# An encoder block on one core: the next head's transposes moved ahead of the value products in each attention step

## The chip, the core and the metric

The kernel runs on one core of a Trainium2 chip. Its time is the device time of one execution in microseconds; smaller is better. A core has TensorE (matmuls and transposes), VectorE, ScalarE, GpSimd and queues that issue DMAs; they run side by side and wait for one another by semaphores. In the profile TensorE is PE (its weight loads PEld), VectorE DVE, ScalarE ACT, GpSimd POOL, and the queue of the sync engine SP.

## What is computed

One layer of a bidirectional encoder over two request groups (1024 and 256 tokens, width 1024, all float32), each attending to itself alone:

```
p = rmsnorm(x) @ w_in                         # uv, c_q, c_kv, k_rope, gate_A, gate_B
A = chunked gMLP of uv;  B = attention of 8 heads from c_q, c_kv, k_rope
    s = q @ k.T * 192**-0.5;  prob = softmax(s);  o = prob @ v        # per head
x = x + (sigmoid(gate_A) * A + sigmoid(gate_B) * B) @ w_out
x = x + expert_choice_ffn(rmsnorm(x))         # 16 experts
```

A head has 128 plain and 64 rotated dimensions for queries and keys and 128 for values. The change concerns the attention alone.

## The kernel before

Every product is made in float32 precision from two parts of each operand, a high one (rounded) and a low one (what the rounding left): three matmuls, high by high, high by low and low by high. So each operand that comes out of a transpose is copied by ScalarE (high part), and VectorE subtracts this from the original in PSUM (low part).

The attention stage is a loop of 84 steps, written out by hand in the same order on each engine; the engines' orders are fixed. Step n belongs to head h = n // 10 and to the query chunk of 128 tokens ORD[s], s = n % 10, with ORD = (0, 1, 2, 3, 8, 9, 4, 5, 6, 7). Chunks 0 to 7 are the first group, with 1024 keys; 8 and 9, at s = 4 and 5, are the second, with 256. In one step TensorE does, in this order:

- `scores(n)`: the scores of step n, ten matmuls of 512 columns (five of 256 at s = 4 and 5), lines L1235 to L1239, into banks 0-1 or 2-3 of PSUM. It waits for the exponential of step n - 2, and at s = 0 for all pieces of its head.
- `turn_prob(n - 2)`: eight transposes (two for a chunk of the second group) of the probabilities of step n - 2, L1248, into bank 4 on. It waits for GpSimd's normalisation of step n - 2 (norm_pool) and for VectorE's low part of step n - 3 (pt_lo_dve).
- `values((n - 4) // 2, n % 2)`: half of the value products of a pair of chunks, 12 matmuls of 256 columns (3 for the pair of the second group, at s = 8 and 9), L371 to L373, into bank 6. The first half waits for the pair's low parts and for the copy of the pair before.
- `turn_head(9 * (h + 1) + s)` for s up to 8 and all heads but the last: one of nine pieces of the next head's queries and keys, two or four transposes, L1181, from the tile tok. All of them write bank 7, so each waits until the high and the low part of the piece before have been made (x_hi, x_lo). s = 0 to 2 are the queries, 3 to 5 the keys, 6 to 8 the rotated parts of both.

After the last step of a head's pieces (s = 8) the SP queue loads tok with the queries (L623) and keys and values (L626) of the head after.

ScalarE in one step: `high(n - 2)`, the high part of the transposed probabilities (L1797); `expo(n)`, the exponential with its sum (L1807); at odd steps `out_pair`, the copy of a finished pair of value products (L1814); then `high_head`, the high part of the step's piece (L1761, for rotated ones L1764, L1765 and L1767).
VectorE: `top(n)`, maximum and bias of the scores (L2173, L2175); `low(n - 2)`, the low part of the transposed probabilities (L2182); `inverse(n)`, the reciprocal of the sum (L2188); then `low_head`, the low part of the step's piece (L2131, for rotated ones L2136 and L2138).
GpSimd: the normalisation of the probabilities (L877) from the reciprocal, and at s = 4 the splitting of the next head's values.

Of the kernel before, what the change touches and what calls it, by code (L numbers as in the profile page):

```python
# [33 lines left out]
H = 8  # L34
# [24 lines left out]
PIECES = 9  # L59
# [30 lines left out]
def piece(x):  # L90

    return (0, 2, 1)[x // 3], 4 * (x % 3), (4, 4, 2)[x % 3]
# [22 lines left out]
def keys(c):  # L115
    return (0, TP) if c < NCH_P else (TP, TS)


def build(nc, x_p, x_s, norm1_g, w_in, v_norm_g, w_spatial, b_spatial, w_a_out, q_norm_g, w_uq,
# [3 lines left out]
    with ctx:  # L123
# [24 lines left out]
        def bank(b, n=BANK, w=1):  # L148
            return PS[:, b * BANK:b * BANK + n * w]
# [145 lines left out]
        with ExitStack() as s:  # L295
# [3 lines left out]
            with ExitStack() as s2:  # L299
                sb(s2, "act_room", [P, 2, KD, T])  # L300
                s = s2
# [4 lines left out]
            with ExitStack() as s2:  # L306
                s = s2
# [154 lines left out]
        def x_bank(x):  # L462
            return bank(6 + x % 2 if x < PIECES else 7)
# [525 lines left out]
        def _(pe):  # L989
# [177 lines left out]
            def turn_head(x):  # L1167

                h, i = divmod(x, PIECES)
                kind, c0, cn = piece(i)  # L1170
                pe.wait_ge(S["tq_in"], 16 * (h + 1))
                if kind > 0:
                    pe.wait_ge(S["tkv_in"], 16 * (h + 1))
                free = x - 1 if h == 0 else x
                if h == 0:
                    pe.wait_ge(S["pa_copy"], UNITS)
                if free > 0:
                    pe.wait_ge(S["x_hi"], free)
                    pe.wait_ge(S["x_lo"], free)
                for c in range(cn):  # L1180
                    last = pe.transpose(x_bank(x)[:, c * P:(c + 1) * P],  # L1181
                                        tok[:, c0 + c, (0, NOPE, HEAD + ROPE)[kind]:][:, 0:P], ident[:])
                last.then_inc(S["x_pe"], 1)
# [34 lines left out]
            def scores(n):  # L1218
                h, s = divmod(n, NCH)
                hd, c = heads[h % 2], ORD[s]  # L1220
                k0, kn = keys(c)
                if s == 0:
                    if h < 2:
                        pe.wait_ge(S["krl_zero"], h + 1)
                    pe.wait_ge(S["x_hi"], PIECES * (h + 1))
                    pe.wait_ge(S["x_lo"], PIECES * (h + 1))
                if n > 1:
                    pe.wait_ge(S["exp_act"], n - 1)
                else:
                    pe.wait_ge(S["evac"], 3 * G_B - (3 if n == 0 else 0))  # L1230
                q = slice(c * P, (c + 1) * P)
                for o in range(0, kn, BANK):
                    w = min(BANK, kn - o)
                    out, k = bank(s_bank(n) + o // BANK, w), slice(k0 + o, k0 + o + w)
                    pe.matmul(out, hd["q_hi"][:, q], hd["k_hi"][:, k], start=True, stop=False)  # L1235
                    pe.matmul(out, hd["q_hi"][:, q], hd["k_lo"][:, k], start=False, stop=False)  # L1236
                    pe.matmul(out, hd["q_lo"][:, q], hd["k_hi"][:, k], start=False, stop=False)  # L1237
                    pe.matmul(out, hd["qr2"][:, q], hd["kr2"][:, k], start=False, stop=False)  # L1238
                    last = pe.matmul(out, hd["qr2"][:, q], hd["krl"][:, k], start=False, stop=True)  # L1239
                last.then_inc(S["scores_pe"], 1)  # L1240

            def turn_prob(n):
                kn = keys(ORD[n % NCH])[1]
                pe.wait_ge(S["norm_pool"], n + 1)
                if n > 0:
                    pe.wait_ge(S["pt_lo_dve"], n)
                for k in range(kn // P):
                    last = pe.transpose(bank(4, kn)[:, k * P:(k + 1) * P], prob[:, n % 3, k * P:(k + 1) * P], ident[:])  # L1248
                last.then_inc(S["probT_pe"], 1)

            def values(pr, half):
                h = pr // 5
                hd = heads[h % 2]
                k0, kn = keys(ORD[2 * (pr % 5)])
                ks = kn // P // 2
                if half == 0:
                    pe.wait_ge(S["pt_lo_dve"], 2 * pr + 2)
                    if pr % 5 == 0:
                        pe.wait_ge(S["v_lo_pool"], h + 1)
                    if pr > 0:  # L1260
                        pe.wait_ge(S["values_act"], pr)
                for k in range(half * ks, (half + 1) * ks):
                    v = slice(k0 + k * P, k0 + (k + 1) * P)
                    last = mm3(pe, bank(6, 2 * P), hd["v_hi"][:, v], hd["v_lo"][:, v], pt_hi[:, pr % 2, k],
                               pt_lo[:, pr % 2, k], k == 0, k == 2 * ks - 1)
                if half:
                    last.then_inc(S["values_pe"], 1)

            def b_row(j, k):

                if k == 0:
                    pe.wait_ge(S["w_split"], G_B + j + 1)
                    pe.wait_ge(S["exp_act"], STEPS)
                    if j == 1:
                        pe.wait_ge(S["pt_lo_dve"], STEPS)
                pe.wait_ge(S["part_lo"], at("part_lo", KD + k + 1))
                for b, (t0, tn) in enumerate(BLOCKS):
                    last = mm3(pe, lin_set(j, b), w_hi[:, j, k], w_lo[:, j, k], o_hl[:, k, 0, t0:t0 + tn],
                               o_hl[:, k, 1, t0:t0 + tn], k == 0, k == KD - 1)
                    if k == KD - 1:  # L1280
                        last.then_inc(S["tile_pe"], 1)

            for n in range(STEPS + 4):
                h, s = divmod(n, NCH)
                if n < STEPS:
                    scores(n)
                if 2 <= n < STEPS + 2:
                    turn_prob(n - 2)
                if n >= 4:
                    values((n - 4) // 2, n % 2)  # L1290
                if h < H - 1 and s < PIECES:
                    turn_head(PIECES * (h + 1) + s)
                if n >= STEPS:
                    b_row(0, n - STEPS)
            for k in range(4):
# [1202 lines left out]
```

## Time and profile before

| | |
|---|---|
| time, median of 3 runs | 2140.59 us (2136.91 to 2142.15) |
| span of the profiled execution, first to last instruction | 2139.5 us (no other time of it is given) |
| TensorE busy | 2098.5 us, 98% of the span |
| VectorE, ScalarE, GpSimd busy | 57%, 44%, 31% |
| attention stage | about 752 to 1112 us |

Times in the profile are counted from the start of the span. Busy time is the time in which an engine executes; matmuls overlap one another in the records, so a matmul's own duration is longer than the distance to the next. The chain that ended last is better for distances: there each piece begins where the work moves on to it. The granted clock is the share of TensorE's full speed (2.4 GHz) that it was given in a stretch; the lower of its two levels is 1.2 GHz. "<-" in a row of a tile stands between what is written and what is read; [0.28 <-PE ...] at the end of a row is the idle time before it and who ended it.

### The profile page before, as it was taken

How to read it: one execution, taken by the hardware profiler on the slowest of the kernel's cores; microseconds unless marked ns; L12 is line 12 of the kernel's file. 1: busy time of each engine (PE TensorE's matmuls, PEld its weight loads, DVE VectorE, ACT ScalarE, POOL GpSimd, SP SyncE). 2: the span in 40 equal slices, each digit the busy share in tenths (PEclk: the TensorE clock that was granted, in tenths of full speed). 3: DMA queues.
4: the chain of work that ended last, by engine and by line, in shares of the span. 5: the costliest groups of instructions: out<-in, count | busy, mean ns of one | idle time of the engine just before them, and what ended most of it. 6: DMA issues, size and time to landing. Idle time of an engine off the chain costs nothing.

```text
span 2139.5 us, 33534 instructions
## 1 busy us (share of the span) xinstructions
PE 2098.5 (98%) x13424; PEld 1727.8 (81%) x13424; DVE 1222.6 (57%) x1434; ACT 939.8 (44%) x1180; POOL 670.2 (31%) x434
## 2 busy tenths in 40 slices
PE   8999999999999999999999999899999999999997
PEld 8888888888888888888888888677777777777775
DVE  5344601222385567777654438966667676666764
ACT  5112311211455366666640022355555555555553
POOL 2333222212355366766642510221121111112111
PEclk9999999999999999999999999999999999999999
DMA  5122223544676642213134432588788887877883
GB/s 180 54 88 87 71 103 121 167 131 146 209 262 235 214 143 84 67 65 114 40 101 150 169 119 92 226 341 315 282 292 298 292 311 289 310 286 288 300 291 94
DMA packets 185270, 397.41 MB, mean 186 GB/s; under 512 B 16736, under 2 KB 104800, under 8 KB 185184
## 3 DMA queue, kind: packets, MB, share of 16 engines
q1 hardware_dynamic: 170592, 343.78, 45.1%
q0 software_dynamic: 7680, 20.98, 4.0%
q10 hardware_dynamic: 6912, 31.46, 3.7%
q8 instruction: 60, 0.98, 0.2%
q14 instruction: 26, 0.21, 0.0%
HBM read 317.53 MB, written 78.64 MB: 185 GB/s over the span
## 4 chain that ended last, share of the span: by engine, by line
PE 88%; DVE 7%; ACT 2%; DMA 1%; issue 1%; POOL 0%; SPq 0%; ACTq 0%; DVEq 0%; POOLq 0%
PE PS L1441 25%; PE PS L371 14%; PE PS L372 14%; PE PS L373 14%; PE PS L1472 8%; PE PS L1248 2%; DVE small L2173 1%; PE PS L1235 1%; PE PS L1239 1%; PE PS L1238 1%; PE PS L1236 1%; PE PS L1237 1%; PE PS L1181 1%; ACT prob L1807 1%; PE PS L1140 1%
## 5 line engine op out<-in xcount | busy, mean ns | idle before, releaser
L371 PE MATMUL PS<-act_hi,w_hi 128*128 128x512 f32 (+1 forms) x1072 | 382.7, 357 | 0.3 <-DVE act_lo L1980 0.2
L373 PE MATMUL PS<-act_hi,w_lo 128*128 128x512 f32 (+1 forms) x1072 | 375.5, 350 | 0.0
L372 PE MATMUL PS<-act_lo,w_hi 128*128 128x512 f32 (+1 forms) x1072 | 375.2, 350 | 0.0
L877 POOL TENSOR_SCALAR prob<-prob,small 128x1024 f32<-128x1024 f32 (+1 forms) x80 | 200.4, 2505 | 120.9 <-DVE small L2188 120.9
L371 PEld LDWEIGHTS PS<-act_hi,w_hi 128*128 128x128 f32 x1072 | 202.7, 189 | 27.0 <-issue 0.7
L373 PEld LDWEIGHTS PS<-act_hi,w_lo 128*128 128x128 f32 x1072 | 202.4, 189 | 27.2
L372 PEld LDWEIGHTS PS<-act_lo,w_hi 128*128 128x128 f32 x1072 | 202.9, 189 | 25.2 <-issue 0.7
L780 POOL TENSOR_SCALAR w_hi<-w_raw 128x1024 fp32r<-128x1024 f32 x46 | 49.4, 1074 | 418.5 <-PE PS L373 391.5
L1441 PE MATMUL PS<-ehi,xT_hi 128*128 128x512 f32 x520 | 167.9, 404 | 0.6 <-DVE xT_lo L2370 0.4
L1441 PE MATMUL PS<-elo,xT_hi 128*128 128x512 f32 x520 | 160.8, 390 | 0.0
L1441 PE MATMUL PS<-ehi,xT_lo 128*128 128x512 f32 x520 | 160.6, 390 | 0.0
L947 POOL DMA_INDIRECT y_s<-ob_s,ixs_s x16 | 44.0, 2751 | 354.4 <-DVE ob_s L2456 354.4
L2402 DVE TENSOR_TENSOR elo<-raw,ehi 128x2048 fp32r<-128x2048 f32 x65 | 147.4, 2286 | 11.3 <-ACT ehi L1902 11.3
L1902 ACT ACTIVATE ehi<-raw 128x2048 fp32r<-128x2048 f32 x68 | 129.7, 1911 | 25.6 <-PE PS L1441 16.8
L2051 DVE SCALAR_TENSOR_TENSOR yt<-PS,small,bb 128x512 f32<-128x512 f32 (+1 forms) x24 | 15.9, 662 | 214.2 <-PE PS L1140 214.2
L782 POOL TENSOR_TENSOR w_lo<-w_raw,w_hi 128x1024 fp32r<-128x1024 f32 x46 | 124.7, 2712 | 3.8
L1441 PEld LDWEIGHTS PS<-ehi,xT_hi 128*128 128x128 f32 x520 | 92.4, 188 | 35.3 <-issue 13.2
L2402 DVE TENSOR_TENSOR elo<-raw_w,ehi 128x2048 fp32r<-128x2048 f32 x32 | 72.0, 2289 | 79.4 <-ACT ehi L1902 79.3
L1441 PEld LDWEIGHTS PS<-elo,xT_hi 128*128 128x128 f32 x520 | 97.6, 188 | 21.2
L1441 PEld LDWEIGHTS PS<-ehi,xT_lo 128*128 128x128 f32 x520 | 97.6, 188 | 21.0
L1797 ACT ACTIVATE pt_hi<-PS 128x1024 fp32r<-128x1024 f32 (+1 forms) x80 | 71.9, 898 | 88.8 <-PE PS L1248 87.7
L1628 ACT ACTIVATE stg<-PS 128x512 f32<-128x512 f32 (+1 forms) x48 | 25.3, 527 | 178.3 <-PE PS L373 178.2
(344 smaller groups left out, 4812.2 us busy)
## 6 DMA issues: line engine op xcount, KB each, us to landing
raw<-in_w_gate SPq DMA_DIRECT2D x64, 1024.0 KB, 10.5
raw_more<-in_w_up SPq DMA_DIRECT2D x32, 1024.0 KB, 6.8
raw_w<-in_w_up SPq DMA_DIRECT2D x32, 1024.0 KB, 10.7
w_raw<-in_w_in SPq DMA_DIRECT2D x35, 512.0 KB, 4.0
w_raw<-in_w_down SPq DMA_DIRECT2D x15, 1024.0 KB, 5.0
stg<-in_w_down SPq DMA_DIRECT2D x15, 1024.0 KB, 7.0
gt<-in_w_down SPq DMA_DIRECT2D x15, 1024.0 KB, 11.5
raw_end<-in_w_down SPq DMA_DIRECT2D x15, 1024.0 KB
```

What stands on the lines that cost most here:

```text
L371: pe.matmul(out, lh, rh, start=first, stop=False)
L372: pe.matmul(out, lh, rl, start=False, stop=False)
L373: return pe.matmul(out, ll, rh, start=False, stop=last)
L780: pool.tensor_scalar(w_hi[:, j], w_raw[:, j], 1.0, 0.0, ALU.mult, ALU.add).then_inc(S["w_rounded"], 1)
L782: pool.tensor_tensor(w_lo[:, j], w_raw[:, j], f32(w_hi[:, j]), ALU.subtract).then_inc(S["w_split"], 1)
L877: pool.tensor_scalar(prob[:, n % 3, 0:kn], prob[:, n % 3, 0:kn], prec[:, s:s + 1], None, ALU.mult).then_inc(S["norm_pool"], 1)
L947: pool.indirect_dma_start(y_quarters, bass.IndirectOffsetOnAxis(ap=ixs_s[:, 0:1], axis=0), ob_s[:], None, compute_op=ALU.add).then_inc(S[" ...
L1441: last = pe.matmul(bank(b0 + half), lhs[:, k], rhs[:, pt, kin, half * BANK:(half + 1) * BANK], start=st, stop=sp_)
L1472: last = pe.matmul(bank(bs)[CAP_S * g:CAP_S * (g + 1), 0:GN], few(k), raws[slot][:, k % 2, g * GN:(g + 1) * GN], start=(k == 0), stop=(k = ...
L1797: act.activation(pt_hi[:, pr % 2, 0:kn // P, o:o + P], bank(4, kn).rearrange("p (k q) -> p k q", q=P), ACT.Copy).then_inc(S["pt_hi_act"], 1)
L1902: act.activation(ehi[:, pt], raws[slot], ACT.Copy).then_inc(S["e_hi"], 1)
L2402: dve.tensor_tensor(elo[:, pt], raws[slot], f32(ehi[:, pt]), ALU.subtract).then_inc(S["e_lo"], 1)
```

## The change

In each step `turn_head` is issued directly behind `turn_prob`, ahead of `values`, instead of behind it. Nothing else is changed: the orders of ScalarE, VectorE, GpSimd and the queues are the same, and so are all waits, buffers and sizes.

```diff
                 if 2 <= n < STEPS + 2:
                     turn_prob(n - 2)
+                if h < H - 1 and s < PIECES:
+                    turn_head(PIECES * (h + 1) + s)
                 if n >= 4:
                     values((n - 4) // 2, n % 2)
-                if h < H - 1 and s < PIECES:
-                    turn_head(PIECES * (h + 1) + s)
                 if n >= STEPS:
                     b_row(0, n - STEPS)
```

## Rows read from the trace of the kernel before

**Rows 1.** The page: the span, busy us of each engine (share) xinstructions.

```profile
span 2139.5 us, 33534 instructions
...
PE 2098.5 (98%) x13424; PEld 1727.8 (81%) x13424; DVE 1222.6 (57%) x1434; ACT 939.8 (44%) x1180; POOL 670.2 (31%) x434
```

**Rows 2.** Busy us by stretch: PE, PEld, DVE, ACT, POOL, then granted clock, DMA.

```profile
830.00:870.00 40.00, 39.85 (x272) 35.62 (x271) 29.65 (x49) 26.59 (x46) 27.14 (x12) 1.00 0.35 109
...
1070.00:1080.00 10.00, 8.53 (x69) 8.03 (x67) 6.93 (x12) 7.06 (x12) 6.02 (x3) 1.00 0.26 80
...
1095.00:1100.00 5.00, 3.45 (x21) 3.48 (x22) 2.58 (x3) 2.63 (x5) 3.85 (x2) 0.75 0.44 134
1100.00:1105.00 5.00, 5.00 (x33) 4.55 (x33) 0.73 (x1) 1.39 (x3) 0.00 (x0) 0.91 0.07 27
```

**Rows 3.** The chain that ended last, 804 to 819 us: start, us, what.

```profile
804.58 0.87 PE PS L1248 x8
...
812.73 1.06 PE PS L1248 x8
...
815.23 0.44 PE PS L1181 x4
...
816.26 1.06 PE PS L1248 x8
...
818.76 0.22 PE PS L1181 x2
```

**Rows 4.** The same chain, 824 to 840 us.

```profile
827.34 0.44 PE PS L1181 x4
...
830.08 0.87 PE PS L1248 x8
...
831.31 0.30 PE PS L1181 x2
...
833.91 0.99 PE PS L1248 x8
...
835.25 0.36 PE PS L1235
...
837.82 1.07 PE PS L1248 x8
```

**Rows 5.** Timeline of VectorE, 791 to 838 us: start, us, instruction.

```profile
803.54 0.75 DVE L2131 SCALAR_TENSOR_TENSOR q_lo<-PS,small,q_hi 128x512 fp32r<-128x512 f32 x1 [0.69 <-ACT q_hi L1761]
...
813.40 0.75 DVE L2131 SCALAR_TENSOR_TENSOR k_lo<-PS,small,k_hi 128x512 fp32r<-128x512 f32 x1 [0.69 <-ACT k_hi L1761]
...
814.89 1.22 DVE L2182 TENSOR_TENSOR pt_lo<-PS,pt_hi 128x1024 fp32r<-128x1024 f32 x1 [0.16 <-ACT pt_hi L1797]
...
816.42 0.75 DVE L2131 SCALAR_TENSOR_TENSOR k_lo<-PS,small,k_hi 128x512 fp32r<-128x512 f32 x1 [0.24 <-ACT k_hi L1761]
...
825.35 0.69 DVE L2138 TENSOR_TENSOR krl<-PS,kr 64x512 fp32r<-64x512 f32 x1
...
830.36 0.69 DVE L2138 TENSOR_TENSOR krl<-PS,kr 64x512 fp32r<-64x512 f32 x1
...
834.62 0.43 DVE L2138 TENSOR_TENSOR krl<-PS,kr 64x256 fp32r<-64x256 f32 x1
...
836.46 1.21 DVE L2182 TENSOR_TENSOR pt_lo<-PS,pt_hi 128x1024 fp32r<-128x1024 f32 x1
```

**Rows 6.** Timeline of ScalarE, 791 to 838 us.

```profile
812.67 0.70 ACT L1761 ACTIVATE k_hi<-PS,small 128x512 fp32r<-128x512 f32 x1
...
815.70 0.69 ACT L1761 ACTIVATE k_hi<-PS,small 128x512 fp32r<-128x512 f32 x1 [0.28 <-PE PS L1181]
```

**Rows 7.** Timeline of the SP queue, 740 to 1110 us.

```profile
831.64 0.52 SPq L623 DMA_DIRECT2D tok<-q_d  x1
...
1005.73 0.52 SPq L623 DMA_DIRECT2D tok<-q_d  x1
```

**Rows 8.** DMA issues, 831 to 838 us: count, KB each, us to landing.

```profile
tok<-q_d SPq DMA_DIRECT2D x1, 960.0 KB, 5.5
```

## The prediction

> **What bounds the kernel now.** I read the page first: TensorE is busy for 98% of a span of 2139.5 us [rows 1]. So the change can pay only where TensorE waits inside the attention stage (about 752 to 1112 us), and costs where it puts a wait into a full TensorE. The table by stretch comes next: from 830 to 870 us TensorE was busy for 39.85 of 40 us at a granted clock of 1.00, while VectorE had 29.65 and ScalarE 26.59 us [rows 2]. There is almost nothing to win there. But the other engines' handovers can lie close to TensorE's needs, which an average doesn't show, so I followed the chain of work through one head (h = 1, 796 to 840 us) and put beside it the timelines of VectorE and ScalarE. "Step s" is the position in the head, n = 10h + s; P are the transposes of the probabilities, V the value products, T the next head's transposes, S the scores.
>
> In the chain a row starts when TensorE's work moves on to it. Eight transposes take 0.87 us, four T 0.44, two T 0.22 [rows 3, 4]. The V of step 5 fills 817.32 (816.26 + 1.06) to 818.76, 1.44 us for 12 matmuls; a V of the small pair, steps 8 and 9, fills 830.95 (830.08 + 0.87) to 831.31, 0.36 us.
>
> A handover from VectorE to a transpose is to be seen at step 5: the low part of the probabilities ended at 814.89 + 1.22 = 816.11 [rows 5], P began at 816.26 and took 1.06 instead of 0.87 us [rows 3]. So from the end of the producer to the place from which normal pace counts it is 0.15 + 0.19 = 0.34 us. At step 0 of the next head: 836.46 + 1.21 = 837.67, P from 837.82 with 1.07 us [rows 4, 5], 0.35. I use 0.34.
>
> **The change part by part.** No instruction is added or removed, no bytes, no buffer. T moves past V: 12 matmuls, 3 at steps 8 and 9 (step 9 has no T), and nothing at steps 0 to 3 of head 0, where there is no V. TensorE's sum per step stays: P + T + V + S has the same parts. What moves is the moment at which T's waits must be met: T of step s waits until VectorE has written the low part of the piece before (x_lo), because all pieces share one PSUM bank. Until now V's 1.43 us lay ahead of that wait as cover; now only P does. V behind T waits for low parts that P's own wait has met already, and for the copy of the pair before; both are done. The SP queue: the load of the next head's queries starts when T of step 8 is done, and T of step 0 needs it. It was issued at 831.64, about 5.5 us to landing [rows 7, 8], so some 837.1; T will stand behind P of step 0, which ends at 837.82 + 1.07 = 838.89 [rows 4]. Still covered by 1.7 us. T of the key kinds needs the second load only from step 3. At step 2 T may begin at 803.54 + 0.75 + 0.34 = 804.63 [rows 5], and P ends at 804.58 + 0.87 = 805.45 [rows 3]; of the steps 0 to 3 this has the least to spare. ScalarE and GpSimd: the copy of T's result comes behind the exponential of its step, and at odd steps behind the copy of V's result too, so a T that ends earlier gives ScalarE little: at step 3 the copy of the keys (812.67) follows without a gap behind ScalarE's own work [rows 6]. V ends later by T's 0.22 to 0.44 us, and nothing waits closely for it.
>
> Now the sum for one head. The low part of a piece ends at 813.40 + 0.75 = 814.15 (step 3), 816.42 + 0.75 = 817.17 (step 4), 825.35 + 0.69 = 826.04 (step 6), 830.36 + 0.69 = 831.05 (step 7), 834.62 + 0.43 = 835.05 (step 8) [rows 5].
>
> Step 4. P ends at 812.73 + 1.06 = 813.79, where T now wants to begin. It may at 814.15 + 0.34 = 814.49. New wait: 0.70 us. Before, T stood at 815.23 [rows 3], later than 814.49, so V hid the wait with 0.74 us to spare. This low part is late because ScalarE's copy was, whose input was there long before; so moving T of step 3 earlier doesn't mend it.
>
> Step 5. T of step 4 now ends at 814.93. Its copy began at 815.70, for which ScalarE had idled 0.28 us [rows 6], and can begin some 0.3 us earlier; its low part earlier by the 0.24 us that VectorE idled for it [rows 5], 816.93. TensorE is late by 0.70, so P can start at 816.26 + 0.70 = 816.96, when the low part that it waited for (816.11, plus 0.34) is long there: its 1.06 shrinks to 0.87. I round what it gives back to 0.20; shift after P: 0.70 - 0.20 = 0.50. P ends at 817.32 + 0.50 = 817.82, and T may begin at 816.93 + 0.34 = 817.27: no new wait. Everything behind, the scores, maxima and exponentials of steps 6 and 7 too, is now late by 0.50.
>
> Step 7. P ends where V began, 827.34 - 1.43 = 825.91, with the shift 826.41. T may begin at 826.04 + 0.50 + 0.34 = 826.88. New wait: 0.47; shift 0.97. The low part of step 7 hangs on the exponential and on VectorE's order, not on this wait, so it stays late by 0.50 only.
>
> Step 8. P ends at 830.95 + 0.97 = 831.92, T may begin at 831.05 + 0.50 + 0.34 = 831.89: no new wait. T took 0.30 instead of 0.22 us [rows 4], which falls away: shift 0.89. Step 9: P took 0.99 instead of 0.87: shift 0.77. Step 0: the first score product took 0.36 us instead of 0.23, a tenth of the 2.30 from 831.61 (831.31 + 0.30) to 833.91; it waits for the last low part. Shift 0.64. Then P of step 0: TensorE is ready at 837.68 + 0.64 = 838.32 (835.25 + 0.36 + 9 x 0.23 = 837.68), the low part at 837.67 + 0.50 + 0.34 = 838.51: the old wait shrinks from 0.33 to 0.19 us, and the shift becomes 0.50 again. So the wait of step 7 is paid back by the tail of the head, where VectorE's chain sets the pace, and what remains of a head is step 4's wait less what step 5 gives back: 0.70 - 0.20 = 0.50 us. The head repeats: the query loads stand at 831.64 and, four heads later, at 1005.73, 43.52 us apart each [rows 7]. T is issued in the heads 0 to 6, and steps 4 to 8 exist with V in all seven: 7 x 0.50 = **3.5 us**.
>
> Bounds. Step 4's wait: not under 0 (it is hidden if the copy comes 0.7 us earlier than I think), and at most 0.70 with nothing given back, 4.9 us in all. Steps 4 and 7 with nothing given back: 7 x (0.70 + 0.47) = 8.2 us. All places where T's cover shrinks below its need, singly and with nothing given back: 0.70 at step 4, at step 5 what is short from the old times, 817.17 + 0.34 - 817.32 = 0.19, at step 7 826.38 - 825.91 = 0.47, at step 8 831.39 - 830.95 = 0.44 less the 0.08 of today: 1.72 x 7 = 12.0 us. The waits of V (two semaphores, at even steps) now stand behind only two to four transposes. The trace has no such place; the nearest is S behind two transposes with one wait, and there T's row is the plain 0.22 us [rows 3], with no gap behind it. I take nothing; at the upper end a slow first product of 0.19 us as above, at 4 even steps with T behind P and V in each head, 7 x 4 x 0.19 = 5.3 us. A gain: at most the waits of today, 0.20 + 0.20 + 0.08 + 0.12 + 0.13 + 0.33 = 1.06 us in a head (steps 4, 5, 8, 9 and 0), 7.4 us if all go and none comes; step 4's own is ahead of T, and takes 1.4 of it off.
>
> The clock. At step 4 TensorE will do, between the scores and V (P began at 812.73 [rows 3]), only transposes or nothing: 1.05 + 0.70 + 0.44 = 2.19 us. The trace holds a fall: between 1095 and 1100 us the granted clock averages 0.75, between 1100 and 1105 0.91, and of the first of them TensorE was busy for 3.45 of 5 us; between 1070 and 1080, with 1.47 us idle in two waits, it stayed at 1.00 [rows 2]. 0.75 and 0.91 mean 2.5 + 0.9 us at the lower level (1.2 GHz), which cost half of that, 1.7 us. The Trainium skill (page "TensorE: Matmul & The Clock Gate", Part 4: PE-mode transpose) says that the full clock does not engage for transposes, which speaks against lining up P, the wait and T; by that rule the sum would be the clock rival's below. The row from 1070 to 1080 speaks for 3.5 us, the fall shows that the rival is not impossible.
>
> **The rivals.**
> A (forecast): one new wait of 0.70 us at step 4 and one of 0.47 at step 7, the latter absorbed: +3.5 us, 2144.1. Chance 0.60.
> B: hidden anyway. ScalarE's copies come earlier with T and no low part is late: 2140.6. For it speaks the 0.28 us idle of ScalarE at step 4; against it that at step 3 ScalarE isn't waiting for T. 0.13.
> C: nothing is absorbed, or V's waits show. +8.2 to +12.0 us, 2148.8 to 2152.6. For it: the margins are tenths of a microsecond. Against: the tail of each head waits for VectorE today. 0.15.
> D: the clock falls once per head at step 4: 3.5 + 7 x 1.7 = 15.4, 2156.0. 0.05.
> E (the other side): the pieces finish earlier and VectorE's backlog at the head's end, where the low parts of step 8 end at 835.05 only and hold the scores and P of step 0, is gone, with no new wait: 7 x (0.08 + 0.12 + 0.13 + 0.33) = 4.6 us, 2136.0. It decides from the point where the copy at step 8 follows T, not the exponential, and where step 3's low part ends before 813.45. Against it: both rows say otherwise. 0.07.
>
> **How the numbers follow.** The sum was made against the profiled execution (span 2139.5 us; no other time of it is given), 1.1 us under the median of the three runs, 2140.59; 2139.5 + 3.5 = 2143.0, and carried over to the median 2144.1. The runs shown differ by 5.2 us, so the median of a few may be off by some 2 us. The range 2138.0 to 2151.5 takes in A, B and most of C; outside are D, most of E and the end of C. About 0.3% (6.4 us) is what a measurement of this kernel tells from no change. A and B are inside it but for a small part of A on the slow side; of C most is beyond, D wholly; of E hardly anything by its own price. Faster 0.03, the same 0.78, slower 0.19.
>
> **What would show it.** In the profile of the changed kernel: TensorE idle ahead of T, released by the low part of the keys, at step 4 of each of seven heads for about 0.7 us and at step 7 for about 0.45; none at steps 0 to 3, 5 and 6; P of step 5 back at 0.87 us; query loads some 44.0 us apart instead of 43.52; clock 1.00 throughout; no wait of T on the query load. The prediction is wrong if T waits at step 4 are absent (B), if the heads are 44.6 us or more apart (C), if the clock falls (D), or if they are under 43.4 apart (E).

## The result, and the profile after

The changed kernel takes 2145.28 us (median of 11 runs, 2142.30 to 2147.08), the kernel before 2140.47 us (11 runs): a ratio of 1.0023, interval 1.0015 to 1.0030, so 3.2 to 6.4 us slower. Run again beside the kernel before in a later set of runs (e8) it was 1.0028 (1.0019 to 1.0037). Forecast were +3.5 us and 2144.1.

The loads of the next head's queries (SP queue: start, us) mark the heads:

```profile
792.55 0.52 SPq L623 DMA_DIRECT2D tok<-q_d  x1
...
836.56 0.52 SPq L623 DMA_DIRECT2D tok<-q_d  x1
...
1012.63 0.52 SPq L623 DMA_DIRECT2D tok<-q_d  x1
```

From 836.56 to 1012.63 lie four heads of 44.02 us; before they were 43.52 us apart [rows 7]. So a head takes 0.50 us longer, and seven make 3.5 us. The whole stage says the same. From the first of its query loads to a store near its end, before and then after, are 332.22 and 335.64 us, 3.4 us more:

```profile
747.72 0.52 SPq L623 DMA_DIRECT2D tok<-q_d  x1
...
1079.94 0.32 SPq L639 DMA_DIRECT2D o_d<-ostg  x1
```

```profile
751.65 0.52 SPq L623 DMA_DIRECT2D tok<-q_d  x1
...
1087.29 0.32 SPq L639 DMA_DIRECT2D o_d<-ostg  x1
```

The distance of the heads is a far finer gauge than the time of the kernel: it is a difference inside one execution, between places that the rest of the kernel doesn't touch.

Where the half microsecond is, the timeline of the head shows that [rows 3 to 6] show (h = 1; start, us, instruction, idle before it and its end). First step 4:

```profile
817.07 0.70 ACT L1761 ACTIVATE k_hi<-PS,small 128x512 fp32r<-128x512 f32 x1
817.13 1.06 PE L1248 MATMUL PS<-ident,prob 128*128 128x128 f32 x8
...
817.80 0.75 DVE L2131 SCALAR_TENSOR_TENSOR k_lo<-PS,small,k_hi 128x512 fp32r<-128x512 f32 x1 [0.69 <-ACT k_hi L1761]
...
818.69 0.63 PE L1181 MATMUL PS<-ident,tok 128*128 128x128 f32 x4 [0.50 <-DVE k_lo L2131]
```

P ends at 817.13 + 1.06 = 818.19. The low part of step 3's piece ends at 817.80 + 0.75 = 818.55, 0.36 us later, and T begins at 818.69 after 0.50 us of idle TensorE, and then takes 0.63 us where it took 0.44 [rows 3]. Together 0.50 + 0.19 = 0.69 us, on a TensorE that had none of it before. The chain that ended last then goes on so (start, us, what):

```profile
818.69 0.63 PE PS L1181 x4
...
821.35 0.87 PE PS L1248 x8
...
822.23 0.22 PE PS L1181 x2
...
831.08 0.63 PE PS L1181 x4
...
835.43 0.87 PE PS L1248 x8
...
836.31 0.22 PE PS L1181 x2
...
839.17 0.87 PE PS L1248 x8
...
840.40 0.23 PE PS L1235
...
842.49 0.23 PE PS L1239
842.71 1.06 PE PS L1248 x8
...
843.77 0.44 PE PS L1181 x4
```

Line by line against [rows 3, 4]: P of step 5 is back from 1.06 to 0.87 us. T of step 7 takes 0.63 instead of 0.44, a wait. T of step 8 is back from 0.30 to 0.22, P of step 9 from 0.99 to 0.87. The first score product of the next head is back from 0.36 to 0.23. P of step 0 is still a waiting one with 1.06, but it follows the last score product without a gap (842.49 + 0.23), where 0.13 us lay before (837.69 to 837.82). Together 0.08 + 0.12 + 0.13 + 0.13 = 0.46 us, nearly all that step 7's wait had cost.

All seven heads do the same, as the table of who waited for whom over the stage (752 to 1118 us; us in total, times, longest) says. None of the L1181 rows is in the table of before:

```profile
PE PS L1181 <- DVE k_lo L2131: 3.5, 7, 0.5
PE PS L1181 <- DVE krl L2138: 2.0, 7, 0.3
```

Seven waits of 0.50 for the keys' low part (step 4), and seven of 0.28 for that of the rotated parts (step 7). The slower first transposes, 0.19 each, come on top.

Outside the stage the two profiled executions differ for another reason. The query load at the stage's beginning stands at 751.65 instead of 747.72, 3.9 us late before any edited instruction has run. In the table by stretch (busy us of PE, PEld, DVE, ACT, POOL, then the granted clock and DMA) the changed kernel's execution has

```profile
300.00:310.00 10.00, 10.00 (x52) 8.24 (x51) 0.00 (x0) 1.16 (x3) 0.00 (x0) 0.83 0.01 2
600.00:610.00 10.00, 8.25 (x35) 7.42 (x36) 6.96 (x20) 6.66 (x15) 1.27 (x2) 0.83 0.77 263
1095.00:1105.00 10.00, 7.89 (x51) 6.75 (x50) 7.08 (x10) 7.11 (x12) 7.98 (x4) 1.00 0.06 19
```

and that of before

```profile
300.00:310.00 10.00, 10.00 (x63) 8.61 (x62) 0.00 (x0) 1.75 (x4) 0.00 (x0) 1.00 0.01 2
600.00:610.00 10.00, 8.55 (x44) 7.08 (x43) 4.84 (x15) 5.66 (x12) 1.08 (x2) 1.00 0.73 251
1095.00:1105.00 10.00, 8.45 (x52) 8.03 (x53) 3.31 (x4) 4.02 (x8) 3.85 (x2) 0.83 0.26 80
```

A mean of 0.83 over 10 us is 3.4 us at the lower level (1.2 GHz), an estimated 1.7 us lost. Such a fall comes at 304 and 602 us in one execution, at 1097 us in the other. The same DMA issues in both executions, taken as marks, say what they came to. The changed kernel's are level with the others before 304 us, 1.6 us late behind it, 3.9 late at the stage's beginning, 7.35 late at the store near its end (1079.94 and 1087.29), and 5.8 late behind the fall of the kernel before, from 1105 us on. So 5.9 us between the spans (2145.4 to 2139.5) are not 5.9 us of the change: 3.4 to 3.5 are. And some 0.7 us of the 3.9 are more than the two falls make; e8 below comes back to them.

### The profile page after: what moved, and what is told of

It reads as the page before. It is cut to its first block, busy times and chain, and to the rows that moved or that the text cites. A ratio compares the mean times of both kernels' runs of the same rounds, so it can differ in the third digit from the quotient of the medians.

```text
span 2145.4 us, 33534 instructions
## 1 busy us (share of the span) xinstructions
PE 2099.2 (98%) x13424; PEld 1729.3 (81%) x13424; DVE 1225.6 (57%) x1434; ACT 940.2 (44%) x1180; POOL 672.5 (31%) x434
## 4 chain that ended last, share of the span: by engine, by line
PE 89%; DVE 5%; ACT 2%; issue 1%; DMA 1%; POOL 0%; SPq 0%; ACTq 0%; DVEq 0%; POOLq 0%
PE PS L1441 25%; PE PS L371 14%; PE PS L372 14%; PE PS L373 14%; PE PS L1472 8%; PE PS L1248 2%; PE PS L1239 1%; PE PS L1236 1%; PE PS L1238 1%; PE PS L1235 1%; PE PS L1237 1%; PE PS L1181 1%; ACT prob L1807 1%; PE PS L1140 1%; DMA stg<-ya_d 1%
```

## The experiments

Each theory says what the heads' distance must be. Theory A is the prediction's: step 4's wait is paid, less 0.20 us that step 5 gives back, and step 7's is taken back by the tail of the head. Rival C says that waits add up. Rival O, that the order costs in every step (V behind T's waits, transposes in a row).

**Step 4 alone** (e1_only_4)

```diff
-                if n >= 4:
-                    values((n - 4) // 2, n % 2)
-                if h < H - 1 and s < PIECES:
+                first = s == 4
+                if first and h < H - 1 and s < PIECES:
+                    turn_head(PIECES * (h + 1) + s)
+                if n >= 4:
+                    values((n - 4) // 2, n % 2)
+                if not first and h < H - 1 and s < PIECES:
                     turn_head(PIECES * (h + 1) + s)
```

> The next head's transposes stand ahead of the value products at step 4 of each head alone. Theory A (only step 4's wait is paid): TensorE waits about 0.6 to 0.7 us ahead of them for the keys' low part, step 5 gives 0.20 back, and the query loads of successive heads lie 44.0 us apart, as in the changed kernel (44.02; 43.52 before), +3.5 us in all. Rival C (waits add up, step 7's 0.47 is paid too): without step 7 the distance must be shorter than the changed kernel's, 43.8 or less. Rival O (the order itself costs a little in every step): of 0.50 us in a head about a ninth, distance 43.6.

Measured (SP queue):

```profile
832.59 0.52 SPq L623 DMA_DIRECT2D tok<-q_d  x1
...
1008.57 0.52 SPq L623 DMA_DIRECT2D tok<-q_d  x1
```

Four heads of 43.995 us: one of nine moves brings 0.47 of the 0.50 us (ratio 1.0010, 1.0001 to 1.0020). That rules out C (43.8 or less) and O (43.6).

**All but steps 4 and 5** (e2_not_4_5): the same edit with `first = s not in (4, 5)`.

> The changed order in all steps but 4 and 5. Theory A: no wait at steps 4 and 5; at step 7 TensorE still waits some 0.3 to 0.5 us ahead of the next head's transposes, but the tail of the head takes it back (the wait ahead of the probabilities' transposes at step 0 shrinks), so the query loads lie 43.52 us apart as before, and the time is that of the kernel before within 1 us. Rival C (the wait at step 7 is paid): 44.0. Rival O (the order itself costs): seven ninths of the cost stay, 43.9.

Measured: loads from 831.64 to 1005.85, 43.55 us apart; ratio 0.9997 (0.9987 to 1.0006). And yet TensorE waits in each head, for as long as in the changed kernel:

```profile
PE PS L1181 <- DVE krl L2141: 2.0, 7, 0.3
```

A wait seven times in the table, and 0.03 us of it in the heads' distance: the time is missing from the waits behind it. The chain through the head of [rows 4] has T of step 7 with its wait, then T of step 8 and P of step 9 at their quick 0.22 and 0.87 us:

```profile
826.16 0.63 PE PS L1181 x4
...
831.40 0.22 PE PS L1181 x2
...
834.27 0.87 PE PS L1248 x8
```

**Step 5 alone** (e3_only_5): `first = s == 5`.

> The changed order at step 5 alone. Theory A: the low part of step 4's piece ends at 817.17 and 0.34 later, at 817.51, the transposes may begin; the probabilities' transposes end at 817.32: a wait of 0.19 us that nothing takes back, query loads 43.7 us apart, +1.3 us. Rival B (such small waits vanish in the slack of the other engines): 43.5 us apart. Rival O: about a ninth of the cost, 43.6.

Measured: loads from 833.58 to 1008.28, 43.68 us apart, so 0.16 us in a head, against 0.19 expected. T of step 5 shows it, 0.41 us where [rows 3] have 0.22:

```profile
819.11 0.41 PE PS L1181 x2
```

It is 1.1 us in all, which the time doesn't show (0.9998, 0.9988 to 1.0007).

**The changed order without the shared bank** (e4_own_banks), on the changed kernel:

```diff
         def x_bank(x):
+            if x >= PIECES and x % PIECES in (4, 5):
+                return bank(1 if x % PIECES == 4 else 3)
             return bank(6 + x % 2 if x < PIECES else 7)
...
                 free = x - 1 if h == 0 else x
+                if h > 0 and i in (4, 5, 6):
+                    free = PIECES * h + 4 if i == 6 else 0
...
+                if h < H - 1 and s in (6, 7):
+                    pe.wait_ge(S["x_hi"], PIECES * (h + 1) + s - 1)
+                    pe.wait_ge(S["x_lo"], PIECES * (h + 1) + s - 1)
```

> The changed order in all steps, but the pieces of steps 4 and 5 are written to the PSUM banks 1 and 3, which the short scores of these two steps leave free, so they need not wait for the piece before; the scores of steps 6 and 7 wait instead until these banks have been read. Nothing else differs from the changed kernel. Theory A (the shared bank's wait at step 4 is the whole cost): no wait ahead of these transposes at step 4, query loads 43.5 us apart, the time of the kernel before within 1 us. Rival O (what costs is the order on TensorE, such as the value products behind transposes with their own waits, not the bank): 44.0 us apart, +3.5 us.

Measured: loads from 831.90 to 1005.87, 43.49 us apart; ratio 0.9996 (0.9986 to 1.0006). The wait for k_lo is gone and the cost with it; that for krl (7 times, 2.0 us) stays, unpaid. So it is the one PSUM bank of all pieces that makes the changed order dear. A row that I had not expected, of the weight loads, in the same table:

```profile
PEld PS L1185 <- DMA tok<-q_d: 0.4, 1, 0.4
```

T waited once for the load of its queries, which took 7.3 us; the head from 788.05 to 831.90 is 43.85 us long.

**ScalarE's order, on the changed kernel** (e5_copy_first)

```diff
+                ahead = s % 2 == 1
+                if ahead and h < H - 1 and s < PIECES and n > 0:
+                    high_head(PIECES * (h + 1) + s)
                 if n % 2 and 5 <= n:
                     out_pair((n - 5) // 2)
-                if h < H - 1 and s < PIECES and n > 0:
+                if not ahead and h < H - 1 and s < PIECES and n > 0:
                     high_head(PIECES * (h + 1) + s)
```

> The changed kernel, and at odd steps ScalarE makes the high part of the next head's piece ahead of the copy of the pair's value products instead of behind it. At step 3 the copy of the value products takes about 0.27 us ahead of the keys' high part (812.40 to 812.67 before). Theory A: the keys' low part of step 3 is done 0.27 us earlier, so step 4's wait shrinks from about 0.70 to 0.43 us; further 0.1 us comes back at the tail, where steps 5 and 7 have the same copy. Query loads 43.6 to 43.7 us apart instead of 44.02, +1.4 us to the kernel before. Rival B (the low part is late for another reason, VectorE's order): 44.0, +3.5 us.

Measured: loads from 834.12 to 1008.75, 43.66 us apart; ratio 1.0010 (1.0000 to 1.0019).

```profile
PE PS L1181 <- DVE k_lo L2134: 1.9, 7, 0.5
```

The waits for the keys' low part fell from 3.5 to 1.9 us, 0.23 each. So the copy of the value products, 0.27 us ahead of the high part, is one of the things that make this low part late. The chain of the changed kernel shows the whole of it, ScalarE's exponential, copy and high part in a row:

```profile
815.62 0.97 ACT prob L1807
...
816.71 0.20 ACT prob L1807
816.91 0.27 ACT ostg L1814
817.18 0.59 ACT k_hi L1761
```

**Steps 7 and 8 of the kernel before** (e6_order_by_step): T ahead of V with `first = s == 8`, the high part ahead with `ahead = s == 7`. **All odd steps on ScalarE, TensorE as before** (e7_before_copy_first): `ahead = s % 2 == 1` on the kernel before.

> The kernel before with two edits only: at step 8 the next head's transposes stand ahead of the value products, and at step 7 ScalarE makes the high part of the piece ahead of the copy of the value products. Theory A: the tail of a head is paced by ScalarE and VectorE (exponential, high part, low part of steps 7 and 8, then the probabilities' low part), so 0.27 us taken out of this chain at step 7 comes back in the waits of steps 9 and 0: query loads 43.2 to 43.3 us apart instead of 43.52, -1.9 us in all, under what the time itself can tell. Rival (TensorE is the bound there too, the tail's waits are handover only): 43.5.

> The kernel before with TensorE's order unchanged; only ScalarE's order changes, at all odd steps: the high part of the piece ahead of the copy of the value products. Theory A: the same 0.27 us at the tail, but the transposes of these steps end 0.44 us behind the value products, so ScalarE waits for them and the copy of the value products comes later; the next pair's first product waits for it at step 8. Query loads 43.2 to 43.4 us apart, -1.3 us. Rival: 43.5 us apart.

Measured: 43.25 us apart (830.34 to 1003.35) and 43.37 (831.04 to 1004.52); ratios 0.9983 (0.9974 to 0.9992) and 0.9986 (0.9976 to 0.9995). The distances are those forecast; the medians are 3.2 and 3.4 us under that of before, where the heads make 7 x 0.27 = 1.9 and 7 x 0.15 = 1.1 us. Only the heads' part is shown to be the edits' own: ahead of the stage, where nothing was edited, both profiled executions are 0.8 us quicker than that of before, and the mean granted clock of e7's runs is 0.9953 against 0.9936 beside them. By their heads both are faster than the kernel before and the changed one. In the second the copy of the value products has become late, as expected:

```profile
PEld PS L371 <- issue: 3.1, 7, 0.5
```

```profile
PE PS L371 <- ACT ostg L1814: 1.7, 7, 0.2
```

**The changed kernel again** (e8_change_again), unedited, and **own banks with ScalarE's new order** (e9_banks_copy_first), the edits of e4 and e5 together:

> The changed kernel once more, beside the kernel before on one chip, for the size of the time difference: 4.8 us was measured where the heads' distance accounts for 3.5. Theory A (the heads are all of it): query loads 44.0 us apart, ratio about 1.0016, and what is above is the spread of the granted clock outside the attention stage. Rival (a second cost behind or ahead of the stage belongs to the change): ratio 1.0023 or more again, with the same stretch outside the heads longer in this profile.

> The changed order, with the pieces of steps 4 and 5 in banks of their own as in the earlier run, and ScalarE's order of the earlier run (the high part of the piece ahead of the copy of the value products at odd steps). Theory A: neither step 4's nor step 5's wait is there, step 7's (0.4 us) is, and the tail is 0.1 us shorter: query loads 43.3 to 43.4 us apart, -0.7 us to -1 us. So the changed order is no better than the old one even without its wait, only the shorter chain on ScalarE is. Rival (the changed order helps once the bank is out of the way): clearly under the 43.25 us of the variant with the order chosen by step.

Measured for the first: loads from 833.39 to 1009.44, 44.01 us apart; ratio 1.0028 (1.0019 to 1.0037). The heads repeat to a hundredth, and so does the stage, from its first query load to the store near its end (335.64 us again):

```profile
748.46 0.52 SPq L623 DMA_DIRECT2D tok<-q_d  x1
...
1084.10 0.32 SPq L639 DMA_DIRECT2D o_d<-ostg  x1
```

But the time is above what they account for, and here 1.0016 lies outside the interval. The mean granted clock of its 11 runs is 0.99345, that of the 21 runs of before beside them 0.99405; 0.0006 of 2140 us is 1.3 us, and the means of the runs (2145.6 and 2140.4) less that differ by 3.9 us. So part of what lies beyond the heads may be time at the lower clock, at most 1.3 us of it, since not every stretch at the lower clock costs time (1370 to 1380 us, at the document's end). Whether the change brings it about or these runs happened to have more of it, they don't decide.

As to the rival, behind the stage nothing is added: the execution is 4.16 us late at the store near the stage's end and 4.2 at an issue at 1276 us. Ahead of the stage there is a stretch that no edit touches and that is longer, between two loads of w_a_out, first before, then here:

```profile
576.48 1.01 SPq L479 DMA_DIRECT2D w_raw<-in_w_a_out  x1
...
631.43 1.01 SPq L479 DMA_DIRECT2D w_raw<-in_w_a_out  x1
```

```profile
576.54 0.98 SPq L479 DMA_DIRECT2D w_raw<-in_w_a_out  x1
...
632.18 0.98 SPq L479 DMA_DIRECT2D w_raw<-in_w_a_out  x1
```

It takes 54.95 us before and 55.64 here with the clock at 1.00, and in the changed kernel's first profile 57.3 with one fall, again 0.7 more than the fall's 1.7. In e6 and e7 it takes 54.1 and 54.2, in the others 54.6 to 55.1. So 0.7 us of what the heads don't account for is seen in both executions of the changed kernel. Why isn't known, and one or two profiles of a kernel don't tell whether it belongs to the kernel or to the execution.

Measured for the second: 43.42 us from 831.29 to 874.71 and 43.43 on to 918.14, and 43.41 at the end, near the expected 43.3 to 43.4. But between 918.14 and 962.56 lies a head of 44.42 us. The DMA issues of that stretch (KB, us to landing) and the timeline:

```profile
tok<-q_d SPq DMA_DIRECT2D x1, 960.0 KB, 7.8
```

```profile
925.98 0.66 PE L1185 MATMUL PS<-ident,tok 128*128 128x128 f32 x4 [0.70 <-DMA tok<-q_d]
```

The load took 7.8 us instead of 5.5 [rows 8], and T, which stands earlier now, waited for it: 0.70 us of idle. Median ratio 1.0006 (0.9997 to 1.0016). The undisturbed heads are 0.1 us shorter than those of before and 0.2 longer than e6's 43.25, so the rival (that the changed order helps once the bank is out of the way) has nothing for it; and with the late load this version's time isn't below that of the kernel before.

## Why the prediction was right

Its direction and size held. +3.5 us were forecast, the heads give 3.5, the medians 4.8 (3.2 to 6.4), and 5.7 (4.1 to 7.9) in the repeat. The mechanism is the forecast one; the time beyond the heads is not in it.

- Step 4: 0.70 us forecast, 0.69 measured, in the forecast place and with the forecast releaser. The handover of 0.34 us read off other places (0.15 idle and 0.19 slow start) is 0.33 here (818.55 to 818.69, and 0.63 - 0.44).
- Step 5: 0.20 us given back. P's 1.06 is 0.87 again, and e1 has 0.47 us net by itself.
- Step 7: 0.47 us forecast, 0.28 + 0.19 = 0.47 measured, and taken back by steps 8, 9 and 0 (0.30 to 0.22, 0.99 to 0.87, 0.36 to 0.23, and the gap of 0.13 ahead of P of step 0). e2 and e4 keep this wait and cost nothing: shown, where the prediction had argued it.
- Rival B (hidden) fails by the seven waits, C by e1, E by the distance of 44.02. Rival D, the clock: it stays at 1.00 in the heads of both profiles of the changed kernel, with 2.19 us of transposes and waiting in step 4 (the row below is of the first). Near the stage's end, at 1090 to 1110 us, a fall comes in the executions of before, e1, e2, e6, e8 and e9 and not in those of the changed kernel's first profile, e3, e4, e5 and e7. So it goes neither with the change nor against it: e8 is the changed kernel itself. By the marks this fall cost 1.5 us in the execution of before, where the prediction had reckoned 1.7. The Trainium skill (page "TensorE: Matmul & The Clock Gate", Part 4: PE-mode transpose) was one of the reasons for that rival; in these heads, where the clock was up when the transposes came, the trace doesn't bear it out.

```profile
830.00:870.00 40.00, 39.22 (x265) 34.99 (x264) 29.27 (x48) 26.36 (x46) 27.30 (x12) 1.00 0.35 109
```

- "Still covered by 1.7 us", of the query load: for the loads of the median kind yes, for all no. From the issue to T of step 0 it was 840.32 - 831.64 = 8.7 us before (838.89 + 1.43 = 840.32 [rows 4]), and is 843.77 - 836.56 = 7.2 us now. But a load of 7.8 us does occur (e9), and then T waits. Such waits are in the profiles of e4 (0.4 us) and e5 (0.3 us in two) too, not in the two of the changed kernel. The step should have asked for the spread of the load's duration, not its usual value: over the 77 loads of the eleven profiles it is 5.1 to 7.8 us, and six took 7.0 or more.
- The rest, 1.3 to 2.2 us above the heads in the medians, is not explained by any step. Both profiles of the changed kernel have 0.7 us more than that of before ahead of the stage (576 to 631 us), where nothing was edited. Late query loads, which cost up to 1.0 us each where they occur, may be in other executions, and in e8's runs the clock was lower by 0.0006. The other way round, e1's runs are 2.1 us above before in the median, where its heads make 3.3. Its cause stays open.

## What to carry to other kernels

On an engine that is 98% busy, a wait costs nothing only while work stands between the moment at which it would begin and the moment at which it is met. Before moving an instruction ahead, compare, step by step, the end of what it waits for with its new place, handover included; the change measured here costs half a microsecond in one of nine places and nothing in the other eight, though one of these (step 5) would cost 0.16 us by itself. A wait that appears isn't yet a loss: where a slower chain sets the pace further on, it is paid from waits that were there already. And where the time of a whole kernel scatters by more than the edit is worth, measure the distance between two repeated marks inside one execution, over several repeats.

## What the runs showed that I had not expected

The heads' distance, averaged over four heads, repeats to 0.01 us between the two executions of the changed kernel (44.02 and 44.01), while its times range over 5 us. Single heads are less even: 43.40 to 43.65 us in the execution of before, 42.96 to 43.56 in that of e6. What differs between the two executions compared above is where the clock fell while TensorE set the pace (at 304 and 602 us in one, at 1097 us in the other), about 1.6 us each time. Between 1370 and 1380 us it averaged 0.50 in one and 0.83 in the other, and yet the one was late by 5.8 us at 1278 us and by 5.9 at the end: there the clock cost next to nothing. The load of 960 KB in an otherwise quiet stage takes 5.9 us in the median, and 7.8 in one of the heads of the last profile. What lengthens it wasn't looked into.
